# Forget-gate page attention: the decays of both head pairs enter the score banks first

## What is computed

```python
def fox_attention(q, q_pos, k, v, logf):          # 16 q heads, 4 kv heads
    c = jnp.cumsum(logf.astype(F32), axis=1)
    c_k = c.reshape(B, L, G, R).transpose(0, 2, 3, 1)
    ...
        s = jnp.einsum('bqgrd,blgd->bqgrl', qg, kf) + (c_q - c_k[:, None])
        p, _ = masked_softmax(s, ...)
        return (jnp.einsum('bqgrl,blgd->bqgrd', p, vf).reshape(B, Q, H, D),)
```

## Time and profile before

| | us |
|---|---|
| median of 3 runs | 3827.74 (3823.85 to 3831.76) |
| profiled execution, its own time | 3813.61 |
| its span | 3811.8 |
| TensorE busy in the span | 3206.7 (84%) |
| VectorE | 1456.2 (38%) |
| ScalarE | 1003.4 (26%) |
| GpSimd | 580.0 (15%) |
| forget-gate page attention: set-up | about 3143 to 3187 of the span |
| its rounds | 3187 to about 3640 |

### The profile page before, as it was taken

One profiled execution on the slowest core, in us unless ns is written; L12 is line 12 of the kernel. 1 busy time (PEld: TensorE's weight loads), 2 busy tenths in 40 slices (PEclk: granted clock), 3 DMA queues, 4 the chain that ended last, 5 costly groups with the idle time before them and its releaser, 6 DMA issues. The chain is left out here.

```text
span 3811.8 us, 67405 instructions
## 1 busy us (share of the span) xinstructions
PE 3206.7 (84%) x22697; PEld 2138.3 (56%) x22697; DVE 1456.2 (38%) x4231; ACT 1003.4 (26%) x2410; POOL 580.0 (15%) x927
## 2 busy tenths in 40 slices
PE   6899997999999888996655748899768876898869
PEld 5444446988888555553524534466545554565633
DVE  0301101444443355553224547311146654554523
ACT  0100000322322356562102321100035542333311
POOL 0000001222220000002014635000011103332200
PEclk9999998999999599996668989999779997999989
DMA  1455364544442222134337965421452208999732
GB/s 32 148 206 202 135 234 119 140 121 127 123 125 55 69 69 74 54 96 125 154 119 247 300 204 182 140 71 55 135 138 54 67 24 267 330 296 313 260 150 83
DMA packets 341880, 556.86 MB, mean 146 GB/s; under 512 B 74003, under 2 KB 225083, under 8 KB 337899
## 3 DMA queue, kind: packets, MB, share of 16 engines
q1 hardware_dynamic: 265924, 355.43, 30.2%
q0 software_dynamic: 52288, 166.16, 13.6%
q10 hardware_dynamic: 23340, 30.98, 2.3%
HBM read 490.66 MB, written 118.25 MB: 160 GB/s over the span
## 5 line engine op out<-in xcount | busy, mean ns | idle before, releaser
L965 PE MATMUL PS<-cmp_xT,cmp_w 128*128 128x255 f32 (+2 forms) x2176 | 485.9, 374 | 1.1 <-DVEq L1044 1.1
L313 PE MATMUL PS<-even_w,even_xT 128*128 128x512 f32 (+1 forms) x1152 | 476.4, 574 | 1.6 <-DMA even_w<-in_w_in_e 1.6
L965 PEld LDWEIGHTS PS<-cmp_xT,cmp_w 128*128 128x128 f32 x2176 | 392.3, 191 | 47.6 <-issue 1.2
L855 ACT ACTIVATE cmp_xT<-PS 64x512 f32<-64x512 f32 x260 | 155.0, 596 | 868.5 <-PE PS L936 867.0
L313 PEld LDWEIGHTS PS<-even_w,even_xT 128*128 128x128 f32 x1152 | 218.6, 191 | 248.5 <-issue 242.6
L855 DVE COPY cmp_xT<-PS 64x512 f32<-64x512 f32 x260 | 179.3, 689 | 292.3 <-PE PS L936 290.3
L313 PE MATMUL PS<-odd_w,odd_xT 128*128 128x368 f32 x896 | 282.9, 477 | 1.4 <-DVE odd_xT L266 1.4
L313 PEld LDWEIGHTS PS<-odd_w,odd_xT 128*128 128x128 f32 x896 | 170.4, 192 | 107.1 <-issue 4.0
L873 POOL DMA_DIRECT2D cmp_pairs<-in_cache_nsa x256 | 151.6, 599 | 391.3 <-issue 391.3
L273 DVE COPY even_o<-PS 128x512 f32<-128x512 f32 (+3 forms) x81 | 50.3, 622 | 389.5 <-PE PS L313 379.0
L1597 POOL DMA_DIRECT2D s_fox_kv<-in_cache_fox x256 | 137.6, 538 | 314.9 <-issue 281.5
(11 more groups left out here) (434 smaller groups left out, 4766.9 us busy)
## 6 DMA issues: line engine op xcount, KB each, us to landing
s_fox_kv<-in_cache_fox POOLq DMA_DIRECT2D x256, 256.0 KB, 7.4
s_fox_kv<-in_cache_fox SPq DMA_DIRECT2D x256, 256.0 KB, 8.1
cmp_pairs<-in_cache_nsa POOLq DMA_DIRECT2D x256, 128.0 KB, 2.9
cmp_pairs<-in_cache_nsa SPq DMA_DIRECT2D x256, 128.0 KB, 2.9
s_sel_kv<-in_cache_nsa POOLq DMA_DIRECT2D x256, 128.0 KB, 5.0
s_sel_kv<-in_cache_nsa SPq DMA_DIRECT2D x256, 128.0 KB, 5.0
out_dil_sample<-in_cache_dil_w SPq DMA_DIRECT2D x8, 4088.0 KB, 24.4
even_w<-in_w_in_e SPq DMA_DIRECT2D x8, 2048.0 KB, 8.1
```

The lines of the kernel that those rows point to most:

```text
L313: last = nc.tensor.matmul(bank(c, t, 128)[:, 0:n], xT[:, k, t * 128:t * 128 + 128], w[:, c % WS, k, 0:n], start=(k == 0), stop=(k == KT - 1))
L855: last = nc.vector.tensor_copy(dst, x) if l else nc.scalar.activation(dst, x, ACT.Copy)
L965: last = nc.tensor.matmul(hidden_ps(x, NK)[:, g], w1[:, kv, c, :], xT[:, u % 2, kv, g, c % 8, at:at + NK], start=(c == 0), stop=(c == 15))
```

## The change

The decays of both pairs are loaded apart: `dec` gets a dimension for the pair, and `load_decay` issues each of its four DMAs twice. Pair 0 has unit j at partition 32j as before, pair 1 at partition 32((j+1) % 4). Both copies hold the same 16 rows. In `scores` the eight decay matmuls of both pairs come first, alternating between the pairs, and open the accumulation; the query matmuls are added to them. The wait for the decays (`dec_in`) counts double, the wait on `expd` is one for both banks and stands ahead of the decays, and the wait for the copied keys stands behind them. The call for layer 0 computes as before.

```diff
-            dec = sb("dec", [128, 2, RB, KW])
+            dec = sb("dec", [128, 2, P, RB, KW])
...
+        def decay_rows(p, j):
+
+            return 32 * ((j + p) % 4)
+
         def load_decay(eng, b):
             if b >= 2:
                 eng.wait_ge(scored, RB * P * (b - 1))
             v = E.decay[b].rearrange("h (k j n) -> j h k n", k=RB, j=4)
-            for j in range(4):
-                eng.dma_start(dec[32 * j:32 * j + 16, b % 2], v[j]).then_inc(dec_in[b % 2], 16)
+            for p in range(P):
+                for j in range(4):
+                    at = decay_rows(p, j)
+                    eng.dma_start(dec[at:at + 16, b % 2, p], v[j]).then_inc(dec_in[b % 2], 16)
...
                 def scores(r):
                     b = r // RB
+                    if fox:
+                        if r % RB == 0:
+                            hold(dec_in[b % 2], 64 * P * (b // 2 + 1))
+                        hold(expd, r * P)
+                        for j in range(4):
+                            for p in range(P):
+                                rows = slice(decay_rows(p, j), decay_rows(p, j) + 16)
+                                nc.tensor.matmul(PS[32 * j:32 * j + 32, s_bank(r * P + p)], hsel[rows, p, :], dec[rows, b % 2, p, r % RB, :], start=True, stop=False)
                     for e in range(2):
                         hold(tcopied[e], 2 * r + 2)
-                    if fox and r % RB == 0:
-                        hold(dec_in[b % 2], 64 * (b // 2 + 1))
                     for p in range(P):
                         x = r * P + p
-                        hold(expd if fox else s_free, x - 1)
+                        if not fox:
+                            hold(s_free, x - 1)
                         for j in range(4):
-                            last = nc.tensor.matmul(PS[32 * j:32 * j + 32, s_bank(x)], q[:, p, b, :], kT[:, p, j, :], start=True, stop=not fox)
-                        if fox:
-                            for j in range(4):
-                                rows = slice(32 * j, 32 * j + 16)
-                                last = nc.tensor.matmul(PS[32 * j:32 * j + 32, s_bank(x)], hsel[rows, p, :], dec[rows, b % 2, r % RB, :], start=False, stop=True)
+                            last = nc.tensor.matmul(PS[32 * j:32 * j + 32, s_bank(x)], q[:, p, b, :], kT[:, p, j, :], start=not fox, stop=True)
                         last.then_inc(scored, 1)
```

## The result

The changed kernel takes 3843.13 us (median of 7 runs, 3827.89 to 3853.78), the kernel before 3827.74 us beside it (7 runs, 3816.78 to 3843.04): ratio 1.004, interval 1.0021 to 1.0059. That is some 15 us slower, where 3842 us was forecast. The profiled execution of the changed kernel took 3848.22 us, with a span of 3846.6 us and a mean granted clock of 0.902 (before: 3813.61, 3811.8 and 0.916).

What follows compares the result with a forecast made beforehand. The prediction took TensorE and DMA as both near their limits, with DMA the bound after the change: rounds +3, set-up +9, SP's issue +2, so +14 us, 3828 profiled and 3842 us for the runs' median; range 3812 to 3868.

Steps and rivals of the forecast that it cites:

- signs: Trace marks expected: decay group about 0.6 us, page waits 25 to 45 us, DMA share 1.0 and over, first turn about 3192.
- TensorE's 0.53 us a round: TensorE's rounds: overlapping decays and fewer shape changes save 0.53 us a round, 34 us over 64 rounds.
- Rivals 2 and 3: On TensorE: decays don't overlap in a column quarter, +24, 3852, chance 0.08; all eight run serially, +160, 3990, chance 0.03.
- Set-up +9: Stage set-up: two more decay sets delay the first turn by their DMA time, 7.3 to 10.2 us, taken as 9.
- Price of a set: Decay loads in the rounds: DMA time x of one set, bounds 3.65 and 5.1 us, taken as 5.1.
- rival 1: Page loads in the rounds: pages still come in time and the kernel is faster, -25 us, 3803, chance 0.16.
- Lost time of 1.7 us a sequence: Rounds: 1.7 us a sequence added for unusable free DMA time and one clock fall, giving 58.1 us.
- TensorE gives its gain back as waits for pages: Rounds: DMA becomes the bound in all sequences, TensorE's page waits rise from 2.2 to 25 to 45 us.
- Rounds +3: All rounds: five sequences +11, first wait +4, free rounds -12, together +3 us.
- the free rounds: 13 rounds before the first wait and 10 behind the last: 23 at -0.53 us each, -12 us.
- the first wait: Rounds, ahead of the five sequences: TensorE's first wait costs +4 us, about the 5.1 us of a set.
- the 2 us added for SP's longer issue: SP's queue: four more DMA issues at 0.64 us for each of six sets, mostly hidden, +2 us.

Runs made afterwards that it cites:

- e7: Changed kernel without decay loads after sequences 0 and 1, whose decays serve sequences 2 to 7: ratio 0.9944 to the kernel before.
- e1: Kernel before in its old order, with each decay set loaded a second time into rows nothing reads: ratio 1.0081 to the kernel before.
- e10: Changed kernel with each late set's eight transfers spread 3, 3 and 2 over three of SP's page loads: ratio 0.9988 to the kernel before.
- e2: Changed kernel with the second decay copy loaded for sequences 0 and 1 only: ratio 0.9995 to the kernel before.
- a1: Changed kernel profiled a second time, no edit: set-up 49.0 us, rounds 438.6 us.
- e4: Changed kernel with decays of heads 8 to 15 stored 256 keys later, so one copy serves both pairs: ratio 0.9948 to the kernel before.
- e3: Kernel before with both pairs' decays first, in the same row quarter, without a second copy: ratio 1.0003 to the kernel before.
- e13: Changed kernel with each late set's eight transfers in four parts of two: ratio 1.007 to the kernel before.
- e8: Changed kernel with the second decay copy issued from GpSimd's queue, in the rounds one round behind SP's first: ratio 1.0037 to the kernel before.

## Why the prediction was right

*The number* (3842 for 3843.1) *and its signs* came out; one step of its mechanism did not.

- **TensorE's 0.53 us a round**: right, 5.97 to 5.44 us, with a decay group of 0.59 us. Rivals 2 and 3 fall with it: four row quarters write each bank within these 0.59 us. The gain is real: without late sets it shows in full, at 51 us a sequence (e7).
- **Set-up +9**: right, +9.4 and +8.6 us in two pairs of profiles, and e1 shows that the loads alone make it. That is 4.3 to 4.7 us for each of the two sets, more than the 3.65 that the prediction read from three windows (they begin at 3151, 4.5 us behind SP's first decay issue, and leave out what had passed by then). Only the clock time of the first turn (3209.43 for 3192) was off, by low clock in stages ahead.
- **Price of a set**: of the two bounds I took the high one. e10's five sequences behind the first stand at a DMA share of 1.01 to 1.04, about the saturated one, and average 55.0 us, which is what x = 3.65 gave in rival 1; x = 5.1 gave 56.4. So a sequence was over-sized by about 1.4 us. By e7, e2 and e10 a set is 4.1 us of DMA work, and pages alone are 46.7 (the prediction had 46.2).
- **Lost time of 1.7 us a sequence**: under-sized by about 0.6 us. The same five sequences average 57.5 us in after and 57.1 in a1, 2.3 above e10's. The two errors nearly cancel: 57.3 us where 58.1 was forecast. That they do is luck, since what the 1.7 us stood for was one fall of the clock and unused DMA time, and not stops.
- **"TensorE gives its gain back as waits for pages", 25 to 45 us**: this step failed. Page waits are 1.4 us (a1: 6.9 us), and the DMA share of a sequence is 0.94 to 1.01, not 1.0 and over in most of each. The time went into stops of 24.7 us at the ends of instruction lines and into the lower clock at them, 58.0 and 41.0 us of it in the rounds where before had 6.8 and 3.4. Nine of after's 13 stops over 0.5 us, the five longest among them, stand where a decay set passes, so the place was right and what TensorE waits for was not.
- **Rounds +3**: +4.0 us by the means of two profiles each (441.3 and 437.3). By its parts, in the first profile of each: 6.2 us won ahead of the first decay wait (46.3 for 52.6 us), 5.9 lost in the first sequence with a late load (62.3 for 56.4; e7, without the load, still loses 1.3 there), 7.7 lost in the next five, 2.1 won behind them (48.0 for 50.1). Forecast were 12 us won in the free rounds, 4 lost at the first wait and 11 in the five, so the gain and the loss in the five were both too large, the loss at the first wait too small, and the sum about right. With 9 us of set-up these make +13; 2 of the measured 15 us are left over, the size of the 2 us added for SP's longer issue, but no run shows that it is this.
- **Rival 1** (pages in time, faster) described e7 and e4 and not this change: its condition was a price below 2.05 us a set, and 4.1 was measured. Its two sums don't stand on one base: the condition takes pages as 46.2 us, which is 51.3 less 5.1, and the 55.0 us for x = 3.65 add 3.65 to 51.3. With pages at 46.7, as e7 has them, x = 3.65 gives 54.0. That the DMA does bind with two copies, e10 shows: sequences at a share of 1.01 to 1.04 and 55 us.

What stays open: why the instruction lines come late. In seven of the 112 stops, all of 2.7 us or more, the q8 packet began only after TensorE had stopped; in the others it began before, and too late. The packet itself is no slower: 1.14 us in the rounds of after, 1.09 in those of before. So the delay lies ahead of it, and it isn't the bytes alone, since e3 has 10.3 us of stops without them. Open too is how much of the 15 us a fetch that is never late would give back. e10 bounds the rest from one side: with no stop above 2.9 us and 10.2 us of low clock, the same bytes and the same order give a kernel level with before.

## What to carry to other kernels

A gain on TensorE that is paid for with DMA bytes must be counted in both currencies, and where the DMA engines are near a share of 1.0 the same bytes cost more or less by their grouping: eight narrow transfers in a row cost 20 us more here than 3, 3 and 2 (four and four on two queues cost as much as eight). Spreading has its own limit, since a part that comes last in a queue that waits for free slots can be late (e13). Better than either is to ask whether the second copy is needed at all: storing half of the heads 256 keys later made one load serve both pairs, and turned +0.4% into -0.5% (e4).

## What the runs showed of the hardware

- TensorE can stand for up to 4.8 us inside a group of matmuls with no semaphore between them, where it has come to the end of a line of 256 instructions; it goes on 1.2 to 2.1 us behind the end of a 16384-byte packet of the instruction queue (112 stops). The page of the profile shows it only as "issue".
- The granted clock fell to 1.2 GHz within stops of 2.7 to 4.8 us for instructions (those that end at 3281.95, 3344.36 and 3459.82 in after) and of 6.65 us for data (3489.29 in e13); behind the stop of 1.56 us at 3575.28 it fell too. It stayed at 1.00 in e10's sequences from 3305.58 to 3415.57, where no stop under "issue" was longer than 1.02 us.
- Transfers into 16 partitions move 109 GB/s from one queue and 112 to 120 from two at once, most of that time into the same row quarter (e8). Two queues in different halves were not measured for longer than 1.1 us.
- The time ahead of this stage, in code that is the same in before and after, had 548 to 631 us of the lower clock in their four profiles, and the stage's start moved by 26 us (3143.2 to 3169.5). Differences of some 10 us are read from the stage itself, not from the whole.
